# Exponentials of the second attention tile in two sets of four, and a hand-over by halves behind the last expert row

## What is computed

```python
def sliding_window_attention(q, k, v, q_norm_g, k_norm_g, sinks):     # 8 heads
    ...
    p = jax.nn.softmax(jnp.concatenate([s_band, s_meta, sink], axis=-1), axis=-1)
    out = (jnp.einsum('bnhgqk,bnkhd->bnqhgd', p[..., :2 * BLOCK], vb2)
           + jnp.einsum('bnhgqm,bmhd->bnqhgd', p[..., 2 * BLOCK:2 * BLOCK + N_META], v_meta))

def peer_ffn(h, w_query, sub_keys, peer_u, peer_v):                   # 8 heads x 16 experts a token
    ...
        u_sel = peer_u[idx]
        act = jax.nn.gelu(jnp.einsum('chkd,cd->chk', u_sel, hc).astype(jnp.float32),
                          approximate=False) * g
        v_sel = peer_v[idx]
        return jnp.einsum('chk,chkd->cd', act.astype(hc.dtype), v_sel)

    h = h + peer_ffn(rms_norm(h, norm2_g[l]), ...)
    x = even_layer(x, ...)      # rmsnorm, projections, attention, output projection, x + ...
    x = odd_layer(x, ...)
```

## Time and profile before

| | us |
|---|---|
| median of 3 runs | 1200.68 (1197.87 to 1203.76) |
| the profiled execution | 1200.89 |
| its span, first to last instruction | 1199.1 |
| busy: PE, DVE, ACT, GpSimd | 968.8, 734.5, 523.3, 302.7 |
| the rows' stage, first to last dot product | 137.7 to 932.6 |
| gathers | 256, together 270.91 MB |

### The profile page before, as it was taken

One profiled execution on the slowest core, in us unless ns is written; L12 is line 12 of the kernel. 1 busy time (PEld: TensorE's weight loads), 2 busy tenths in 40 slices (PEclk: granted clock), 3 DMA queues, 4 the chain that ended last, 5 costly groups with the idle time before them and its releaser, 6 DMA issues.

```text
span 1199.1 us, 14163 instructions
## 1 busy us (share of the span) xinstructions
PE 968.8 (81%) x4746; PEld 422.2 (35%) x4746; DVE 734.5 (61%) x2007; ACT 523.3 (44%) x1399; POOL 302.7 (25%) x297
## 2 busy tenths in 40 slices
PE   5998977867667677965888878799696698899998
PEld 5665532212222222321222332223241344454564
DVE  5876575689998574657746667666556343242354
ACT  5332259643343542434645564555684213211332
POOL 0000222354445233334422334243234000000000
PEclk9999996778878788977899988899798799899999
DMA  7044898899999999999999999999999765437630
GB/s 302 21 172 174 351 374 300 328 401 419 379 370 388 424 420 424 423 422 421 420 425 424 426 423 378 425 424 418 423 376 385 284 248 191 169 149 280 248 142 19
DMA packets 51737, 395.36 MB, mean 330 GB/s; under 512 B 5536, under 2 KB 10400, under 8 KB 11472
## 3 DMA queue, kind: packets, MB, share of 16 engines
q0 software_dynamic: 37536, 270.91, 55.8%
q1 hardware_dynamic: 13552, 122.83, 25.5%
q10 hardware_dynamic: 576, 0.72, 0.2%
HBM read 393.38 MB, written 1.05 MB: 329 GB/s over the span
## 4 chain that ended last, share of the span: by engine, by line
PE 45%; DMA 20%; DVE 19%; ACT 12%; issue 3%; POOL 0%; DVEq 0%; ACTq 0%; POOLq 0%
DMA expert_rows<-in_peer_uv,peer_idx 19%; PE bank L1825 16%; PE bank L1486 7%; DVE expert_rows L1426 7%; PE bank L1155 4%; ACT L1555 3%; ACT L1464 2%; PE bank L2057 2%; PE bank L2098 2%; DVE r L970 2%; PE bank L1696 1%; ACT peer_diag L1471 1%; PE bank L1732 1%; ACT peer_dots L1465 1%; PE bank L412 1%
## 5 line engine op out<-in xcount | busy, mean ns | idle before, releaser
L1486 PE MATMUL bank<-expert_rows,peer_diag 64*64 64x512 f32 x2048 | 330.4, 735 | 154.1 <-ACT peer_diag L1471 152.7
L1501 POOL DMA_INDIRECT expert_rows<-in_peer_uv,peer_idx x256 | 290.4, 1135 | 526.3 <-PE bank L1486 482.8
L1426 DVE CUSTOM_DVE_ANT_0 expert_rows<-expert_rows,HN 128x1024 f32<-128x1024 f32 x256 | 309.5, 1222 | 134.8 <-DMA expert_rows<-in_peer_uv,peer_idx 133.0
L1825 PE MATMUL bank<-w_ring,b_xt 128*128 128x512 f32 (+1 forms) x576 | 290.0, 624 | 9.5 <-ACT b_sq L1856 4.4
L1464 ACT ACTIVATE peer_dots<-peer_dots 128x1 f32<-128x1 f32 x256 | 51.7, 202 | 321.1 <-DVE peer_dots L1426 319.7
L1486 PEld LDWEIGHTS bank<-expert_rows,peer_diag 64*64 64x64 f32 x2048 | 63.3, 151 | 347.9 <-ACT peer_diag L1471 281.0
L1825 PEld LDWEIGHTS bank<-w_ring,b_xt 128*128 128x128 f32 x576 | 100.5, 196 | 140.8 <-issue 132.1
L1471 ACT ACTIVATE peer_diag<-peer_eyes,peer_dots 128x64 f32<-128x64 f32 x256 | 89.2, 348 | 12.3 <-PE bank L1486 4.0
L1465 ACT ACTIVATE peer_dots<-peer_dots,peer_ex 128x1 f32<-128x1 f32 x256 | 75.6, 295 | 8.3
L1555 ACT ACT_TABLE_LOAD x53 | 68.0, 1283 | 16.9 <-DMA cols<-in_cols 5.7
L1464 ACT ACT_TABLE_LOAD x48 | 61.6, 1283 | 5.3 <-DVE peer_dots L1426 4.4
(11 more groups left out here) (405 smaller groups left out, 1161.4 us busy)
## 6 DMA issues: line engine op xcount, KB each, us to landing
w_ring<-in_w_in_e SPq DMA_DIRECT2D x16, 2048.0 KB, 8.9
w_ring<-in_w_in_o SPq DMA_DIRECT2D x14, 2048.0 KB, 8.8
w_ring<-in_w_query SPq DMA_DIRECT2D x8, 2048.0 KB, 10.6
w_ring<-in_w_out SPq DMA_DIRECT2D x4, 2048.0 KB, 9.6
w_ring<-in_w_out_e SPq DMA_DIRECT2D x4, 2048.0 KB, 9.7
w_ring<-in_w_out_o SPq DMA_DIRECT2D x4, 2048.0 KB
w_ring<-in_w_in SPq DMA_DIRECT2D x2, 2048.0 KB, 20.1
expert_rows<-in_peer_uv,peer_idx POOLq DMA_INDIRECT x256
```

The source lines that it names most:

```text
L1426: t.dve.tensor_tensor_reduce(u, u, t.HN[:, it // PH, :], 1.0, 0.0, ALU.mult, ALU.add, self.dots[:, it, k:k + 1]).then_inc(*self.dotted.add())
L1486: ins = t.pe.matmul(t.PS[2 * T + r][HALF * c:HALF * (c + 1), :], self.diag[tokens, d % self.RD, :], self.slot(n)[tokens, D + c * 512:D + ( ...
L1501: t.pool.indirect_dma_start(self.slot(n), None, t.dram["peer_uv"], bass.IndirectOffsetOnAxis(ap=self.idx[:, it, k:k + 1], axis=0)).then_in ...
L1825: ins = t.pe.matmul(pa[:, 0:n], L.xt[:, k, :], t.w.at(i, k, 0, n), start=k == 0, stop=k == KT - 1)
```

## The change

The exponentials of tile 1's heads 0 to 3 are issued together at step 5, those of heads 4 to 7 and the sink's at step 9. The scores' ring grows from three to six, for which `mT` and `zs` move ahead of it in SBUF; transposes, copies and mixing of a head come three steps later. `finish` takes its quarters column by column. Four 128x128 products into a bank that nobody reads are put ahead of PE's wait for the last row, three more behind it, where PE's wait for the four quarters is dropped. `turn_x` of tile 1 starts its first half behind the first column, into other banks, and `project` starts behind the first half and waits for the second at its fifth slice. Tile 1's result is stored by SP, each tile's stores have a semaphore of their own, and the meta tokens share one with tile 0's tokens.

```diff
     def act():
         t.act.wait_ge(t.constants, 32)
-        t.act.wait_ge(t.tokens[T], 16)
+        t.act.wait_ge(t.tokens[T % 2], (32, 16)[T % 2])
...
-    R = 3
+    R = (3, 6)[T]
...
-    sums, exps, turns, places, mixes = ((0, 1, 2, 3, 4), (1, 2, 3, 4, 5))[T]
+    sums, exps, turns, places, mixes = ((0, 1, 2, 3, 4), (1, 5, 6, 7, 8))[T]
+    at_once = {n + exps: (n,) for n in range(NU)} if T == 0 else {5: range(0, 4), 9: range(4, 8)}
...
-            if exps <= i < NU + exps:
-                n = i - exps
+            for n in at_once.get(i, ()):
                 t.act.wait_ge(*least.at(n + 1))
                 logs(t)
...
-            if i == NU + exps:
+            if i == (NU + exps, 9)[T]:
                 t.act.wait_ge(*sunk.at(1))
...
+def stay_warm(t, n):
+
+    for _ in range(n):
+        t.pe.matmul(t.PS[7][:, 0:P], t.ident[:, :], t.ident[:, :], start=True, stop=True)
...
+HALF_ADDED = 2
+COLUMN_BY_COLUMN = ((0, 0), (1, 0), (0, 1), (1, 1))
...
-        for r, c in QUARTERS:
+        for r, c in COLUMN_BY_COLUMN:
             x = t.X[HALF * r:HALF * (r + 1), T, c * 512:(c + 1) * 512]
...
+                if n == N - 1:
+                    stay_warm(t, 4)
                 t.pe.wait_ge(*self.diagd.at(d + 1))
...
-    banks = (L.pa, L.po)
+    banks = ((L.pa, L.po), (L.po, L.pt))[T]
...
-        t.pe.wait_ge(*L.done["x"])
-        for h, free in ((0, L.free.get(0)), (1, L.po_free)):
+        for h, free in ((0, L.free.get(0)), (1, L.po_free)) if T == 0 else ((0, L.po_free), (1, None)):
+            t.pe.wait_ge(*(L.done["x", 0] if T == 1 and h == 0 else L.done["x"]))
...
+            starts = j == 0 and ("xt", 0) in L.done
+            if starts:
+                t.pe.wait_ge(*L.done.pop(("xt", 0)))
+            elif j == 0:
...
+                if starts and k == 4:
+                    t.pe.wait_ge(*L.done["xt"])
...
-        t.pool.wait_ge(*L.done["x", c])
-        t.pool.dma_start(out[T * P:(T + 1) * P, cols], t.X[:, T, cols]).then_inc(*t.saved.add(16))
+        engine = (t.pool, t.sp)[T]
+        engine.wait_ge(*L.done["x", c])
+        engine.dma_start(out[T * P:(T + 1) * P, cols], t.X[:, T, cols]).then_inc(*t.saved[T].add(16))
...
-    for engine in (t.pe, t.dve, t.act, t.sp, t.pool):
+    stay_warm(t, 3)
+    for engine in (t.dve, t.act, t.sp, t.pool):
         engine.wait_ge(*peer.total.at(QT * len(QUARTERS)))
```

More of the change, by code:

```diff
@@ L1627, in dve @@
                                 bc(t.col(gain)[:, 4 * h:4 * h + 4], P), ALU.mult).then_inc(*placed.add())
-        L.free[0], L.po_free, L.done["xt"] = placed.at(1), placed.at(2), placed.at(2)
+        L.done["xt", 0], L.done["xt"] = placed.at(1), placed.at(2)
+        if T == 0:
+            L.free[0], L.po_free = placed.at(1), placed.at(2)
+        else:
+            L.po_free = placed.at(1)
         yield
@@ L1817, in pe @@
             i = t.w.take(T, matrix, c, n)
-            if j == 0:
+            starts = j == 0 and ("xt", 0) in L.done
+            if starts:
+                t.pe.wait_ge(*L.done.pop(("xt", 0)))
+            elif j == 0:
                 t.pe.wait_ge(*L.done["xt"])
@@ L2601, in both_blocks @@
         t.core.enter_context(t.nc.semaphore(x)) for x in ("constants_in", "late_in", "ssm_in", "keys_in"))
-    t.tokens = [t.core.enter_context(t.nc.semaphore(f"tokens_in{i}")) for i in range(3)]
+    t.tokens = [t.core.enter_context(t.nc.semaphore(f"tokens_in{i}")) for i in range(QT)]
     t.dch, t.ach, t.pch = (Chain(e, t.sem(x)) for e, x in ((t.dve, "dve_chain"), (t.act, "act_chain"),
@@ L2624, in both_blocks @@
     t.zT, t.sg = (area.sb(x, [P, 4, P]) for x in ("zT", "sg"))
+    t.mT, t.zs = (area.sb(x, [P, 4, P]) for x in ("mT", "zs"))
     over = Room(t.nc, start, area.at)
-    as1, pm1 = over.sb("as1", [P, 3, SEQ + META]), over.sb("pm1", [P, PH, META])
-    t.mT, t.zs = (area.sb(x, [P, 4, P]) for x in ("mT", "zs"))
+    as1, pm1 = over.sb("as1", [P, 6, SEQ + META]), over.sb("pm1", [P, PH, META])
     t.small, t.gb = area.sb("small", [P, 15, ST]), area.sb("gb", [P, 4])
@@ L2675, in both_blocks @@
     t.sp.dma_start(t.X[:, 0, :], dram["x"][0:P, :]).then_inc(t.tokens[0], 16)
-    t.sp.dma_start(t.xm[:, :], dram["meta_tokens"]).then_inc(t.tokens[2], 16)
+    t.sp.dma_start(t.xm[:, :], dram["meta_tokens"]).then_inc(t.tokens[0], 16)
     t.w.pump(t.sp)
@@ L2747, in both_blocks @@
     for L, at in zip(lanes, (len(QUARTERS), QT * len(QUARTERS))):
-        L.done["x"] = peer.total.at(at)
+        L.done["x", 0], L.done["x"] = peer.total.at(at - HALF_ADDED), peer.total.at(at)
     lanes[1].other = lanes[0]
@@ L2791, in both_blocks @@
     run(ahead)
-    t.sp.wait_ge(*t.saved.at(32 * QT))
+    for saved in t.saved:
+        t.sp.wait_ge(*saved.at(32))
 def build(nc, dram, out):
@@ L2806, in build @@
         t.area, t.area0 = Room(nc, fixed.at, SBUF_TO), fixed.at
-        t.saved, t.act_set = t.sem("saved"), None
+        t.saved, t.act_set = [t.sem(f"saved{T}") for T in range(QT)], None
         both_blocks(t, dram, out)
```

## The result

The changed kernel takes 1187.74 us as the median of its runs, the kernel before 1201.95 beside it: a ratio of 0.9887, 95% interval 0.9858 to 0.9915, so by this ratio 13.6 us less (10 to 17). The forecast was 17.3 us less.

The account below looks back on a forecast made before the run. ScalarE's table loads were taken to bound tile 1's attention, the DMA the gathers behind it. Savings of 14.0 + 2.0 + 1.3 + 0 = 17.3 us from 1200.89 gave 1183.6 us, range 1176 to 1194.

Parts of the forecast that it names:

- part 1: Tile 1's attention: exponentials in two sets, nine pairs of table loads become two; 14.0 us saved, between 9.4 and 18.0.
- part 2: Hand-over behind the last row: column-by-column finish 1.1 us and unread products 0.9 us; 2.0 us saved, up to 3.7.
- part 4: End of the kernel: storing tile 1 on SP was taken as 0, between a 0.3 us gain and 2.0 loss.
- That excess I leave to the ring: Rows 20 to 28: 8.1 us excess at the attention's end; six slots keep 6 us of lateness from gathers.
- the third that I took of the stretch behind: Hand-over: a raised clock saves a third of 1.5 us in lane 0's transposes and lane 1's first two products.
- Part 3: Tile 1's odd layer: turning x by halves starts its first product earlier; 1.3 us saved, between 1.0 and 1.4.
- Part 5: Kernel start: the first norm also waits for the meta tokens, which land before the constants finish; costs nothing.
- (a): Behind the attention: VectorE sets the pace and 7.5 us of the gain go; 1195.7 us, chance 0.15.
- (b): Tile 1's attention: TensorE at the low clock takes ScalarE's place, 3.3 us a row; 1208.8 us, chance 0.05.
- (c): Hand-over: the clock doesn't rise and lane 0's work fills what the halves free; 1185.6 us, chance 0.13.
- (d): All stages: every gain is kept in full, 23.1 us in all; 1177.8 us, chance 0.07.
- one sign of "wrong": From the last row's products to the end of the span: no less than the present 265.5 us would count against.

Follow-up runs that it names:

- e2: The kernel before with only the exponentials in sets of four and five, the ring of six and the moved mT and zs; 0.9911 of the time before.
- e1: The changed kernel with tile 1's exponentials issued one by one again; 0.9974 of the time before.
- e3: The changed kernel without its seven unread products at the hand-over; 0.9886 of the time before.
- e5: The changed kernel with more unread products at the hand-over: nine instead of three behind the last row, five and 16 behind x's transposes; 0.9882 of the time before.
- e12: The changed kernel measured once more, with the same instructions; 0.9885 of the time before.
- e6: The changed kernel with a further pair of ScalarE table loads in each of the two sets of exponentials; 1192.02 us.
- e4: The changed kernel with VectorE's two additions behind the attention's output projection two rows later, and tile 1's query at pace 0.75; 1184.76 us.
- e10: The changed kernel with e4's later additions and seven, three and nine unread products at the hand-over; 0.9845 of the time before.
- e11: e10 with 14 further unread products where TensorE waits for the last half of tile 0's w_out_o; 1179.32 us.
- e9: The changed kernel with eight unread products ahead of TensorE's wait for each of rows 24 to 29; 1194.66 us.

## Why the prediction came out as it did

It named the direction and the order of the parts, and its range holds the time. The sum was 17.3 us against 13.6; by the stages 10.4 + 1.5 + 1.4 + 0.55 = 13.9. Most of the difference is in the term of part 1; that part 2 came short by as much as part 4 gave over is luck.

**Part 1: 14.0 forecast, 10.7 measured (e2), 10.4 by rows 8 to 34** (83.3 in before and e1, 72.9 on the mean of after, e2, e3, e5, e12). The mechanism was right: table loads behind rows 8 to 16 fell to four, ACT gave way to the DMA, and the halt of a set is paid (e6). Rows 8 to 24 took 44.0 us; 16 rows at 2.51 and the 5.1 us of two halts would be 45.3. What failed is the sentence "That excess I leave to the ring", and with it the step that an advance of the gathers is an advance of the rows. Rows 24 to 34 took 28.5 to 28.9 us before and 28.9 after by the dots, no less, where ten rows at 2.51 are 25.1: 3.8 us.

For the gathers the ring did put the excess off. Counted from their packets in the traces (128 of 8 KB for a row), row 34 landed 83.9 us behind row 8 in before and e1 and 70.2 on the mean of the five, 13.7 less and 0.3 short of the forecast; rows 24 to 34 landed in 25.0 us.

But the dot of row 34 then stood 4.2 to 6.7 us behind its landing, where it had stood 1.7 and 2.0, and the stretch behind has no time to catch up: from 245 to 300 us DVE is busy for 51 to 53 of 55 us in every profile, and at row 72 the dots are 7.0 to 8.1 us behind the landings in all twelve, with or without the change. The DMA moved 401 to 408 GB/s there in the five instead of 414 and 415, and rows 34 to 64 landed in 79.9 us instead of 78.2. At the last row's dot 11.4 us of the gain are left (759.5 from row 8's in before and e1, 748.1 in the five). With the wait out of the dots' way (e4, e10, e11) the dot of row 34 stands 1.1 to 1.2 us behind its landing and the DMA moves 416 to 421 GB/s. So it is shown that the wait makes the dots late; how much of the missing 3 us that is stays open, since next to none of e4's gain is left at the last row.

The excess was in the earlier trace rows already: eight rows in 28.2 us. Its owner was one step further, in the releaser of DVE's idle time there: 2.56 and 2.65 us ahead of the two additions, for the projection's products.

**Part 2: 2.0 forecast, 1.5 measured.** From the last row's products to the last copy, where the halves act, it was 5.7 us before, 4.8 in e3 and 4.4 after (forecast 4.3 to 4.7): by these the halves gave 0.9 where I had 1.1 (e3 is one profile), the clock of the unread products 0.5 more. How the 1.5 us up to the reduction divide isn't shown: e3's last row had the full clock by chance too, and from lane 0's transposes to the reduction it takes 13.8 to 15.1 us in before, e2, e3 and the six profiles with the seven products. What failed is the third that I took of the stretch behind: lane 0's transposes wait 2.23 us for DVE, PE idles, and in after they and lane 1's first two products took 1.11 and 1.91 us, as before. The price of an unread product was wrong as well: it takes 0.52 us at the low clock and not 0.24, so the four ahead of the last row held it back in some profiles. e10 shows what the term can give with the gaps filled by 16 more: 3.7 us. That this is the upper end that I gave for seven is chance.

**Part 3**: 1.3 forecast, 1.4 measured at the odd layer's first product; that they stay to the end isn't shown, as the stage differs by more from profile to profile. **Part 4**: 0 forecast, 0.55 measured, the last addition to the end 2.75 us instead of 3.30, in every profile with the store on SP; its stores landed in 2.0 us. **Part 5**: nothing, and nothing seen.

**The rivals.** (a), given back behind the attention, came in small, for the reason that it gave (DVE has no time left there): 1.8 of the 13.7 us that the gathers had won by row 34 were gone by row 64. By the dots nothing shows, as rows 34 to 255 took 675.3 us against 676.9. (b), PE in ACT's place, did not: rows 8 to 24 fell to 44.0. PE at the low clock did show, but in the projection (5.77 us instead of 3.70), and raising the clock there by unread products made it worse (e9). (c) falls by the hand-over's 1.5 us; e1's interval (0.5 to 5.8 us) would leave room for its 1.3. (d) needed the attention's end to be free.

**The signs.** Right: four loads, the copies 4.4 us behind, the odd layer at 1.34. Missed: the DMA at 382 instead of over 400 in the first stretch, rows at 2.72, row 34's dot at 243.85, the last row's products at 921.40. And one sign of "wrong" came up: 267.5 us from the last row's products to the end, more than the 265.5 of before. It was a bad sign: that stretch holds some 240 us in which the change touches nothing but the odd layer's turn, and whose length moved by up to 6.9 us between profiles with equal instructions. The pair of before and after had it 4.0 us against the change (238.8 and 242.8), about as much as the profiles show less than the medians.

## What to carry to other kernels

When a stage passes from one bound to another, price every wait that stands in the new bound's release path, also those that did not matter before: here two additions queued ahead of the next row's dot. Measure the gain at the engine that sets the pace next: the gathers were 13.7 us early, the dots 10.4. A ring only defers lateness; it absorbs it only if the engine that empties it has time to spare afterwards, and here it had not. Unread products paid in the stages where TensorE had nothing else to do and waited for a known time, in a count that fits the gap; ahead of work that frees buffers they cost more than they gave here (e9).

## What was not expected of the hardware

- One wait of 3.5 to 4.9 us for weights was followed by 6.8 to 10.2 us at a granted clock of 0.50 in every profile that had it, and filling it with 14 unread products (3.3 us) gave 4.3 us of the median beside e10 (their intervals overlap by a little).
- With the same instructions a stage of 240 us took 236.0 to 242.8 us: PE was busy for 219.6 us of it at a mean granted clock of 0.98 and for 226.1 at 0.95, and idle for about the same time.
- An unread 128x128 product took 0.23 us at the full clock (32 instructions in 3.74 us) and 0.52 at half (8 in 2.07).
- The stores from SP at the quiet end landed 2.0 us after their issue.
